# Norm of y behind the gate's panels, and the output projection in four first and four second halves

## What is computed

```python
o_a = rms_norm(o_a, gdn_norm_w) * silu(z_a)              # [512, 1024]
y = ssd_chunked(xs_, dt, a_neg, bm, cm)
y = y + ssd_d[..., None] * xs_
y = y.reshape(bsz, s, SSD_D) * silu(z_s)                 # z_s: columns of h @ w_in
y = rms_norm(y.reshape(bsz, s, SSD_GROUPS, 512), ssd_norm_w)   # two groups of 512 channels
mix = concatenate([o_a, y], axis=-1) @ w_out             # [512, 2048] @ [2048, 1024]
x = x + rms_norm(mix, post_mix_norm)
```

## Time and profile before

| | us |
|---|---|
| median of 3 runs | 2660.88 |
| lowest and highest of them | 2660.53, 2671.55 |
| the profiled execution | 2672.15 |
| its span | 2670.1 |
| TensorE busy | 2512.6 (94% of the span) |
| DVE, ACT busy | 1357.2, 875.4 |

### The profile page before, as it was taken

One profiled execution on the slowest core, in us unless ns is written; L12 is line 12 of the kernel. 1 busy time (PEld: TensorE's weight loads), 2 busy tenths in 40 slices (PEclk: granted clock), 3 DMA queues, 4 the chain that ended last, 5 costly groups with the idle time before them and its releaser, 6 DMA issues.

```text
span 2670.1 us, 32131 instructions
## 1 busy us (share of the span) xinstructions
PE 2512.6 (94%) x13038; PEld 1986.2 (74%) x13038; DVE 1357.2 (51%) x2108; ACT 875.4 (33%) x1453; POOL 120.5 (5%) x156
## 2 busy tenths in 40 slices
PE   8999999997979999999999998888996899999997
PEld 6888888873434888888888887777885688788886
DVE  5444344436773446544533772444364552777723
ACT  4222223222445223322222433433334232433321
POOL 0000000000223000000000000223000000000000
PEclk9999999897789999999999996998997789999998
DMA  5333343210000333333333330000131023233331
GB/s 160 96 102 97 95 120 109 71 52 0 1 1 1 95 96 114 88 100 98 93 101 99 87 81 24 1 2 2 41 88 32 16 71 95 64 102 95 92 100 53
DMA packets 366418, 189.04 MB, mean 71 GB/s; under 512 B 11328, under 2 KB 363840, under 8 KB 366272
## 3 DMA queue, kind: packets, MB, share of 16 engines
q1 hardware_dynamic: 366272, 187.00, 24.4%
HBM read 184.87 MB, written 2.10 MB: 70 GB/s over the span
## 4 chain that ended last, share of the span: by engine, by line
PE 88%; DVE 7%; ACT 3%; issue 1%; POOL 1%; DMA 0%; DVEq 0%; SPq 0%; ACTq 0%
PE ps L407 24%; PE ps L409 24%; PE ps L408 24%; PE ps L653 2%; PE ps L879 2%; PE ps L672 1%; PE ps L913 1%; PE ps L1547 1%; PE ps L787 1%; PE ps L1341 1%; PE ps L1336 1%; PE ps L1331 1%; DVE stat L997 1%; PE ps L519 1%; PE ps L477 1%
## 5 line engine op out<-in xcount | busy, mean ns | idle before, releaser
L407 PE MATMUL ps<-u_hi,w_hi 128*128 128x512 f32 x1968 | 778.9, 396 | 0.9 <-DVE qkv L1467 0.9
L408 PE MATMUL ps<-u_lo,w_hi 128*128 128x512 f32 x1968 | 769.5, 391 | 0.0
L409 PE MATMUL ps<-u_hi,w_lo 128*128 128x512 f32 x1968 | 769.0, 391 | 0.0
L362 DVE TENSOR_TENSOR w_lo<-w_raw,w_hi 128x1024 fp32r<-128x1024 f32 (+2 forms) x366 | 422.7, 1156 | 273.6 <-ACT w_hi L378 272.7
L378 ACT ACTIVATE w_hi<-w_raw 128x1024 fp32r<-128x1024 f32 (+2 forms) x366 | 365.6, 1000 | 447.3 <-PE ps L409 444.0
L407 PEld LDWEIGHTS ps<-u_hi,w_hi 128*128 128x128 f32 x1968 | 368.2, 187 | 87.5 <-issue 4.8
L408 PEld LDWEIGHTS ps<-u_lo,w_hi 128*128 128x128 f32 x1968 | 368.0, 187 | 85.2 <-issue 5.3
L409 PEld LDWEIGHTS ps<-u_hi,w_lo 128*128 128x128 f32 x1968 | 367.8, 187 | 82.2 <-issue 0.9
L409 PE MATMUL ps<-mid_hi,w_lo 128*128 128x512 f32 x528 | 208.6, 395 | 0.0
L407 PE MATMUL ps<-mid_hi,w_hi 128*128 128x512 f32 x528 | 208.6, 395 | 0.0
L408 PE MATMUL ps<-mid_lo,w_hi 128*128 128x512 f32 x528 | 208.5, 395 | 0.0
(11 more groups left out here) (372 smaller groups left out, 2955.1 us busy)
## 6 DMA issues: line engine op xcount, KB each, us to landing
w_raw<-w_in_dram SPq DMA_DIRECT2D x101, 512.0 KB, 3.7
w_raw<-ffn_w_gate_dram SPq DMA_DIRECT2D x44, 512.0 KB, 3.8
w_raw<-ffn_w_up_dram SPq DMA_DIRECT2D x44, 512.0 KB, 3.8
w_raw<-w_up_dram SPq DMA_DIRECT2D x44, 512.0 KB, 3.8
w_raw<-ffn_w_down_dram SPq DMA_DIRECT2D x32, 512.0 KB, 4.2
w_raw<-w_out_dram SPq DMA_DIRECT2D x24, 512.0 KB, 4.1
w_raw<-w_down_dram SPq DMA_DIRECT2D x16, 512.0 KB, 4.0
w_raw<-ffn_w_down_dram SPq DMA_DIRECT2D x16, 384.0 KB, 3.3
```

The lines of the kernel that those rows point to most:

```text
L362: dve.tensor_tensor(lo, raw, hi.bitcast(F32), ALU.subtract).then_inc(w_split, 1)
L407: pe.matmul(out, wh, h_k, start=k0 + k == 0, stop=False)
L408: pe.matmul(out, wh, l_k, start=False, stop=False)
L409: mm = pe.matmul(out, wl, h_k, start=False, stop=end)
```

## The change

1. `gate_act`, for the z projection alone, squares block n - 1 behind the Silu of panel n, and TensorE sums block n - 1 behind z panel n (`z_panel_pe`). Block 7 is squared in `y_norm_act` and summed behind the first panel of the output projection (`out2_panel_pe`), the spread goes behind the second.
2. The passes of the output projection take four first halves into four banks, then four second halves into the same banks. A segment may now carry `parts`, for each panel its bank and first input block. The waits for o_a go block by block, as those for y.
3. The upper parts of o_a are made by ACT, the lower by DVE. The weights' parts for panels 3 to 6 of the output projection are placed by hand into `y_norm_act` and `y_norm_dve`; `upper_part` and `upper_parts` become `upper_to`, which makes all up to a number.

The diff, without the places that only pass the new arguments through:

```diff
@@ -112,12 +112,18 @@
 class Segment:
 
 
-    def __init__(self, name, per, iters, source, blocks, cols, ends):
+    def __init__(self, name, per, iters, source, blocks, cols, ends, parts=None):
         self.name, self.per, self.iters = name, per, iters
         self.source = source
         self.blocks = blocks
         self.cols = cols
         self.ends = ends
+        self.parts = parts
+        if parts is None:
+            self.parts, g, k0 = [], 0, 0
+            for j in range(per):
+                self.parts.append((g, k0))
+                g, k0 = (g + 1, 0) if j in ends else (g, k0 + blocks[j])
         self.base = self.group = 0
 
     def turns(self, eng):
...
@@ -232,7 +238,8 @@
     narrow("ssd_dt", w_in2, S_DT, 16)
     columns("ssd_z", w_in2, S_Z, 4, 2)
     wo2 = kblocks(T["w_out_2"][0])
-    seg("out2", 8, 2, lambda i, j: wo2[:, 8 * (j % 2):8 * (j % 2) + 8, bass.ds(i * (4 * P) + j // 2 * P, P)], [8] * 8, P, [1, 3, 5, 7])
+    seg("out2", 8, 2, lambda i, j: wo2[:, 8 * (j // 4):8 * (j // 4) + 8, bass.ds(i * (4 * P) + j % 4 * P, P)], [8] * 8, P, [4, 5, 6, 7],
+        [(j % 4, 8 * (j // 4)) for j in range(8)])
     wup2 = kblocks(T["w_up_2"][0])
     gate_up("ffn3_up", wup2, wup2, FF)
     down("ffn3_down", kblocks(T["w_down_2"][0]))
@@ -370,18 +377,19 @@
         s = segs[name]
         lower_parts(dve, s.per * s.iters + s.base + LEAD)
 
-    def upper_part(act, n):
-        if n < N_PANELS:
+    raised = [0]
+
+    def upper_to(act, last):
+        for n in range(raised[0], min(last, N_PANELS)):
             blocks, cols = panel_shape[n]
             act.wait_ge(w_landed[n % RING], 16 * (n // RING + 1))
             act.wait_ge(w_used, n + 1)
             act.activation(w_hi[:, n % RING, 0:blocks, 0:cols], w_raw[:, n % RING, 0:blocks, 0:cols], ACT.Copy).then_inc(hi_done, 1)
+        raised[0] = max(raised[0], last)
 
     def upper_parts(act, name, i, g):
         s = segs[name]
-        first = s.ends[g - 1] + 1 if g else 0
-        for j in range(first, s.ends[g] + 1):
-            upper_part(act, i * s.per + s.base + j + LEAD)
+        upper_to(act, i * s.per + s.base + s.ends[g] + 1 + LEAD)
 
     hi_done, cst_in, panels_asked = sem("hi_done"), sem("cst_in"), sem("panels_asked")
 
@@ -390,8 +398,8 @@
 
         s = segs[name]
         for i in s.turns(pe):
-            g, k0 = 0, 0
             for j in range(s.per):
+                g, k0 = s.parts[j]
                 slot = (s.base + j) % RING
                 pe.wait_ge(w_split, i * s.per + (s.base + j + 1 + RING))
                 if k0 == 0:
@@ -408,11 +416,8 @@
                     pe.matmul(out, wh, l_k, start=False, stop=False)
                     mm = pe.matmul(out, wl, h_k, start=False, stop=end)
                 mm.then_inc(w_used, 1)
-                if after and i == 0 and j == 0:
-                    after()
-                k0 += s.blocks[j]
-                if last:
-                    g, k0 = g + 1, 0
+                if after:
+                    after(i * s.per + j)
 
     def sums(eng, name, turns=None):
 
@@ -1477,6 +1482,8 @@
                 gate = pair_a[:, j % 2, :]
                 act.wait_ge(bank_read, read)
                 act.activation(gate, gate, ACT.Silu).then_inc(z_act, 1)
+                if name == "ssd_z" and i * s.per + j:
+                    y_square_act(act, i * s.per + j - 1)
 
     def gate_dve(dve, name, dst, base):
         s = segs[name]
...
@@ -1645,40 +1653,62 @@
             dve.scalar_tensor_tensor(out=x, in0=x, scalar=v(V_SD + b), in1=ps[4 + b % 2][:, :], op0=ALU.mult, op1=ALU.add).then_inc(y_kept, 1)
         dve.wait_ge(y_kept, 8)
 
+    def y_square_act(act, b):
+
+        act.wait_ge(z_dve, 8 + b + 1)
+        if b >= 2:
+            act.wait_ge(y_ss, b - 1)
+        act.activation(pair_b[:, b % 2, :], xbc[:, b, :], ACT.Square).then_inc(y_sq, 1)
+
     def y_norm_act(act):
+        out2 = segs["out2"].base
+        act.wait_ge(w_used, out2 + RING)
         for b in range(8):
-            if b >= 2:
-                act.wait_ge(y_ss, b - 1)
-            else:
-                act.wait_ge(z_dve, 16)
-            act.activation(pair_b[:, b % 2, :], xbc[:, b, :], ACT.Square).then_inc(y_sq, 1)
+            act.activation(u_hi[:, b, :], o_a[:, b, :], ACT.Copy).then_inc(o_upper, 1)
+            if b == 0:
+                y_square_act(act, 7)
+        upper_to(act, out2 + 4)
         for g in range(2):
             act.wait_ge(y_ss, 4 * (g + 1))
             act.activation(stat[:, 56 + 4 * g:60 + 4 * g], ps[6 + g][:, 0:QB], ACT.Sqrt, bias=stat[:, 95:96], scale=1.0 / 512).then_inc(y_rt, 1)
+        upper_to(act, out2 + 5)
         for b in range(8):
             act.wait_ge(y_t, b + 1)
             act.activation(os_hi[:, b, :], pair_a[:, b % 2, :], ACT.Copy).then_inc(y_hi, 1)
-
-    def y_norm_pe(pe):
-        for b in range(8):
-            pe.wait_ge(y_sq, b + 1)
-            for t in range(QB):
-
-                mm = pe.matmul(ps[6 + b // 4][:, t:t + 1], pair_b[:, b % 2, t * P:(t + 1) * P], ones[:, 0:1],
-                               start=b % 4 == 0 and t == 0, stop=b % 4 == 3, skip_group_check=True)
-            mm.then_inc(y_ss, 1)
+            if b % 4 == 3:
+                upper_to(act, out2 + 6 + b // 4)
+
+    def y_sum_pe(pe, b):
+        pe.wait_ge(y_sq, b + 1)
+        for t in range(QB):
+
+            mm = pe.matmul(ps[6 + b // 4][:, t:t + 1], pair_b[:, b % 2, t * P:(t + 1) * P], ones[:, 0:1],
+                           start=b % 4 == 0 and t == 0, stop=b % 4 == 3, skip_group_check=True)
+        mm.then_inc(y_ss, 1)
+
+    def y_spread_pe(pe):
         pe.wait_ge(y_inv, 1)
         for g in range(2):
             spread(pe, ps[4 + g], stat[:, 40 + 4 * g:44 + 4 * g], QB).then_inc(y_bc, 1)
 
+    def z_panel_pe(pe, n):
+        if n:
+            y_sum_pe(pe, n - 1)
+
+    def out2_panel_pe(pe, n):
+        if n == 0:
+            y_sum_pe(pe, 7)
+        elif n == 1:
+            y_spread_pe(pe)
+
     def y_norm_dve(dve, st):
-        dve.wait_ge(z_dve, 16)
-        dve.wait_ge(w_used, segs["ssd_z"].base + 8 + RING)
+        out2 = segs["out2"].base
         for b in range(8):
-            if b == 6:
-                dve.wait_ge(y_rt, 2)
-                dve.reciprocal(stat[:, 40:48], stat[:, 56:64]).then_inc(y_inv, 1)
-            split_dve(dve, st, o_a[:, b, :], u_hi[:, b, :], u_lo[:, b, :], o_ready)
+            dve.wait_ge(o_upper, b + 1)
+            dve.tensor_tensor(u_lo[:, b, :], o_a[:, b, :], u_hi[:, b, :].bitcast(F32), ALU.subtract).then_inc(o_ready, 1)
+        dve.wait_ge(y_rt, 2)
+        dve.reciprocal(stat[:, 40:48], stat[:, 56:64]).then_inc(y_inv, 1)
+        lower_parts(dve, out2 + 4)
         for b in range(9):
             if b < 8:
                 if b >= 2:
@@ -1686,10 +1716,14 @@
                 dve.wait_ge(y_bc, b // 4 + 1)
                 dve.scalar_tensor_tensor(out=pair_a[:, b % 2, :], in0=xbc[:, b, :], scalar=v(V_NORM["ssd"] + b), in1=ps[4 + b // 4][:, :],
                                          op0=ALU.mult, op1=ALU.mult).then_inc(y_t, 1)
+            if b == 0:
+                lower_parts(dve, out2 + 5)
             if b:
                 dve.wait_ge(y_hi, b)
                 dve.tensor_tensor(os_lo[:, b - 1, :], pair_a[:, (b - 1) % 2, :], os_hi[:, b - 1, :].bitcast(F32),
                                   ALU.subtract).then_inc(o_ready, 1)
+            if b in (4, 8):
+                lower_parts(dve, out2 + 5 + b // 4)
         dve.wait_ge(o_ready, 12 + 16)
 
     def post_act(act, name, q, dst):
...
@@ -1855,11 +1889,10 @@
             turn_pe(pe, [xbc[:, b, :] for b in range(10)], 16)
             ssd_pe(pe)
             y_turn_pe(pe)
-            multiply(pe, "ssd_z", u_of(u_hi), u_of(u_lo))
-            y_norm_pe(pe)
+            multiply(pe, "ssd_z", u_of(u_hi), u_of(u_lo), after=lambda n: z_panel_pe(pe, n))
             multiply(pe, "out2", lambda name, j, k: (u_hi[:, k, :] if k < 8 else os_hi[:, k - 8, :]),
                      lambda name, j, k: (u_lo[:, k, :] if k < 8 else os_lo[:, k - 8, :]),
-                     ready=lambda k: pe.wait_ge(o_ready, 12 + 8 + max(0, k - 7)))
+                     ready=lambda k: pe.wait_ge(o_ready, 12 + k + 1), after=lambda n: out2_panel_pe(pe, n))
             post_sum_pe(pe, 5)
             multiply(pe, "ffn3_up", u_of(u_hi), u_of(u_lo), ready=summed_rows_pe(pe, 6))
             multiply(pe, "ffn3_down", u_of(mid_hi), u_of(mid_lo), ready=lambda k: pe.wait_ge(mid_ready, 2 * FK + k + 1))
...
```

More of the change, by code:

```diff
@@ L182, in build, with seg @@
     order = []
-    def seg(name, per, iters, source, blocks, cols, ends):
-        s = Segment(name, per, iters, source, blocks, cols, ends)
+    def seg(name, per, iters, source, blocks, cols, ends, parts=None):
+        s = Segment(name, per, iters, source, blocks, cols, ends, parts)
         s.base = sum(x.per * x.iters for x in order)
@@ L1629, in build @@
     y_inv, y_bc, y_t, y_hi = (sem("y_" + n) for n in ("inverse", "spread", "product", "upper"))
```

(11 more changed lines are left out.)

## The result

The change makes the kernel slower: 2681.56 us in the median of 4 runs (2680.54 to 2687.14) against 2662.75 for the kernel before (4 runs, 2660.53 to 2671.55). The ratio is 1.0069, with a 95% interval of 1.0048 to 1.0089. The profiled execution took 2687.14 us (span 2685.4); the profiled one of before took 2672.15. Four executions of all that follow stand far apart, at 3190 to 13526 us (one each of e1, e2, e5 and of the kernel before beside them); the ratios leave them out, the medians count them.

What follows compares the result with a forecast made beforehand. TensorE, holding 88% of the chain of waits, was taken as the bound. Added 25.2 us plus 11 for the clock, less 20.6 for the norm, gave +15.6: 2676.5 us on the median of 2660.88, range 2663 to 2688.

Steps and rivals of the forecast that it cites:

- The forecast case: Z projection: TensorE stalls between panels and its clock falls behind the stalls; 2676.5 us, chance 0.58.
- stalls: Behind z panels 1 to 7 TensorE waits for a square queued behind the panel's own Silu: 2.15 us each, 15.1 us.
- sums: TensorE's sums of squares, eight blocks at 0.85 us each at full clock: 6.8 us, bounds 6.8 and 12.4.
- spread: Spreading the norm, 16 records between output projection panels 1 and 2, reckoned from 8 in 1.16 us: 2.3 us.
- start of the output projection: TensorE waits for the first parts of o_a made by ACT and DVE: 1.0 us, between 0.5 and 2.
- clock and slow first matmuls: Lower clock behind z panel stalls: five of seven fall at 2.2 us each, +11 us, bounds 0 and 18.
- the norm before: Old norm of y between z and output projections: 19.7 us gap plus 0.9 of slow matmuls, 20.6 us, all removed at best.
- The rival without a stall: Z panels: TensorE's wait for the square is already met, so 15.1 us go; -10.5, 2650.4 us, chance 0.08.
- some will fall: From four head-norm stretches, three ending at clock 0.50, it expected five of seven falls behind z panels.
- The rival in which the clock holds: Z panels: the clock stays up despite the stalls; +4.6 us, 2665.5 us, chance 0.27.
- The upper bound of 12.4: Sums of squares if they run at the lower clock, 1.55 us a block: 12.4 us in all.
- Second halves: Output projection: DVE's chain arrives 3 us early, cost nothing; rival that they are late: +5 us, 2681, chance 0.07.

Runs made afterwards that it cites:

- e1: The change, but ACT takes the square of block n-1 ahead of the Silu of panel n: 2664.44 us median, ratio 0.9978 to the kernel before.
- e2: The change, with eight unused bf16 matmuls on constants ahead of each of the seven waits for a square: 2670.19 us median, ratio 1.0014 to before.
- e5: The change's sums between z panels alone, with the output projection's halves in the old order: 2688.87 us median, ratio 1.0075 to before.
- e3: The change, ACT's order untouched, but TensorE sums block n-2 instead of n-1 behind z panel n: 2663.32 us median, ratio 0.9988 to before.
- r_change_again: The change itself, unedited, run once more beside the kernel before: 2683.58 us median, ratio 1.0071 to before.
- e6: e1 with four sums instead of eight (DVE adds squares) and the first two blocks of o_a's parts made earlier: 2651.56 us median, ratio 0.9952 to before.
- e4: The change's new order of halves alone, with all eight sums in one piece behind z panel 7: 2669.21 us median, ratio 0.9995 to before.

## Why the prediction was right

The forecast case came: stalls at the seven waits, and the clock falling behind them. Its terms against the trace:

| term | predicted | measured |
|---|---|---|
| stalls | 7 x 2.15 = 15.1 | 7 x 2.12 = 14.8 |
| sums | 8 x 0.85 = 6.8 | 7 x 0.91 + 0.81 = 7.2 |
| spread | 2.3 | 1.70 (2207.43 to 2209.13) |
| start of the output projection | 1.0 | 0.42 |
| clock and slow first matmuls | 5 x 2.2 = 11 | 7 x 1.72 = 12.0 |
| sum | 36.2 | 36.1 |
| less the norm before | 20.6 | 20.9 |
| change | +15.6 | +15.2; in the traces +15.5 |

- **The stall.** Its length followed from the old panel's rows to 0.03 us. e1 and e3 show that it hangs on the order on ACT against the wait on TensorE: mending either one removes it. The rival without a stall (2650.4) was decided by reading that order.
- **The clock.** Measured per panel as 10.19 - 5.44 - 2.12 - 0.91 = 1.72 us (panels from 2131.34 to 2141.53). Both factors were off, and in opposite directions: all seven fell where I took five, and each cost 1.72 where I took 2.2, out of 1.4 and 2.6 from the earlier trace rows. That the product came out within 1 us is luck. The step that was mis-sized is the one that read four stretches of the head norms as "some will fall"; those of the earlier trace rows were busy with sums throughout, while two thirds of mine are idle. Not all of the 1.72 is the clock. A panel behind a sum takes 5.56 us in e2, at a clock of 1.00 (8.59 - 2.12 - 0.91), and not the 5.44 of a panel behind a panel, so 0.1 of it goes to a slow start and 1.60 to the clock. By e2 the clock costs 10.8 us in all. The rival in which the clock holds (+4.6, 2665.5) is what e2 is: +4.7 locally.
- **The sums.** 0.91 us at the change's waits, 0.80 where they follow a matmul directly (e1): 0.85 was between them. The upper bound of 12.4 would have needed the sums themselves at the lower clock, and the fall came only behind them.
- **The spread.** The 1.16 us of the earlier trace rows is the length of the merged row; the next operation may start before its end. Reckoned from start to start, as I did for the sums, 16 records cost 1.70, and 2.3 was too much.
- **The start of the output projection.** 0.42 us, just below my 0.5 to 2. Block 0 was ready when reckoned: the first matmul starts 3.46 us after the moment at which the panel could have been followed (2190.38), where I had 3.5. The half microsecond for the last square didn't come; its place between the first two upper parts held nothing up.
- **The norm before.** I counted six matmuls up to 2185.03, but that is the start of the sixth, so five lie ahead of it: 2.28 - 5 x 0.23 = 1.1 us and not 0.9, and the norm cost 20.9 us. With it the terms add up to +15.2; the other 0.3 of the +15.5 I haven't separated.
- **Second halves.** No wait at 2220.13; the DVE chain was hidden, as reckoned.
- **Profiled one against the median.** 2687.8 was forecast for a profiled successor, 2687.14 came. The median was forecast as 2676.5 and is 2681.56, 5 us more: the step that failed is to carry the 11 us between the profiled execution and the median of before over to the change. Its runs lie only 5.6 us below its profiled one. Of the 5 us, 1.9 come from the median of before itself, which a fourth run moved from 2660.88 to 2662.75. That the profiled one was hit within 1 us is luck too: the next section shows how far apart executions of one kernel begin the changed stretch.

## What the runs showed that I had not expected

**The scatter arises in the attention stage, 1000 us before the change.** e3 and r_change_again ran on the same chip and differ only behind 2110 us. Their traces agree up to the projection before attention (first matmul on um_hi at 448.9 and 449.3) and part behind it: the first matmul on mix_hi is at 1067.4 in e3 and 1051.5 in r_change_again, 15.9 us apart, and at 1058.6 before. The window from 700 to 860 us, first before, then r_change_again, then e3, has the granted clock at 0.91, 0.96 and 0.85:

```profile
700.00:860.00 160.00, 138.51 (x513) 64.66 (x512) 99.83 (x330) 75.52 (x221) 49.40 (x70) 0.91 0.00 1
```
```profile
700.00:860.00 160.00, 138.03 (x540) 67.83 (x540) 98.91 (x327) 77.26 (x224) 48.73 (x70) 0.96 0.00 1
```
```profile
700.00:860.00 160.00, 139.69 (x481) 64.22 (x481) 98.22 (x324) 70.61 (x210) 46.81 (x67) 0.85 0.00 1
```

With the higher clock more matmuls are done in the same 160 us (540 against 481). The nine profiled executions reach the z projection between 2110.69 and 2127.68, 17 us apart, as far as the runs of one kernel scatter, and the clock in this window sorts them: at 0.95 or 0.96 (r_change_again, e1, e2, e5, e6) they reach it at 2110.7 to 2111.7, at 0.91 (before, the change) at 2119.4 and 2118.2, at 0.85 (e3, e4) at 2126.9 and 2127.7. The 11 us that the prediction couldn't place are of that size and so are probably no property of the changed stretch; the unprofiled runs have no trace that could prove it run by run. Which of attention's many short waits brings the clock down in a given execution I have not tested. It means that with four to twelve runs a median can be off by several microseconds: e3 is 7.4 us better than before locally and shows a ratio of only 0.9988, which is 3.2 us.

**A short sum alone did no harm here.** 0.80 us of one-column matmuls every 6.39 us left the clock at 1.00 in e1 from 2118 to 2160 us, where 2.12 us idle ahead of 0.91 of them brought it down seven times in seven. One case lies in between: in e6 two sums in a row (1.70 us from 2156.29), six matmuls and 1.20 us of idle time left it at 1.00. In e4, where the sums run without a gap from 2173.44 to 2185.35, the clock is at 1.00 up to 2176 and at 0.50 from there on, and they didn't bring it back. By e2 the falls of the change need the idle time; whether they need the sum behind it as well no run shows.

## What to carry to other kernels

"One step behind" on an in-order engine is only worth something if the old step's instruction also stands ahead of the new step's wait: look at what the instruction queues behind, not at its index. When an idle stretch like this one (2.1 us, and 0.9 us of small sums behind it) recurs between dense matmuls, cost it with the lower clock behind it (here 1.6 us on top of 3.0), and try first to make the stretch shorter. And when runs scatter by more than the change is worth, compare the span of the changed stretch in the traces beside the medians.
